# A transformer's root mean square norms: the root taken straight from the bank of the sums

## The chip, the cores and the metric

The kernel runs on one core of one Trainium2 chip. The metric is the device time of one execution in microseconds, as a median of several runs. TensorE does the matrix products, VectorE and ScalarE the elementwise work, GpSimd (POOL in the profile) some more of it, and SyncE (SP) issues most DMAs.

## The reference

One sequence of T = 512 tokens with D = 1024 features goes through three blocks, all in float32.

1. A first block: adaptive scale, shift and gate vectors from `c`; sliding window attention beside a gated short convolution, each with a norm of its own; an output projection; then a feed-forward part (FFN) with a convolution in its gate, and a norm at the end.
2. An RWKV-7 time mixing block and a SwiGLU FFN, each between two norms.
3. A block with a spatial gate (SGU) and a SwiGLU FFN, each between two norms.

Every norm over features is the same, with EPS = RMS_EPS = 1e-6:

```python
def rms_norm(x, g):
    xf = x.astype(jnp.float32)
    y = xf * lax.rsqrt(jnp.mean(xf * xf, axis=-1, keepdims=True) + EPS)
    return (y * g.astype(jnp.float32)).astype(x.dtype)
```

## The kernel before

**Layout.** The features lie on the 128 partitions, the tokens along the free dimension. An activation is a set of KD = 8 tiles of 128 by 512. Weights come as units of 128 output columns: `load` (L214) brings a unit into `raw`, `split_hi` (L226, ScalarE) rounds it into `whi`, `split_lo` (L232, VectorE) takes the rest into `wlo`, and TensorE makes three products for each tile (L247, L248, L249: high by high, high by low, low by high). Two slots of `whi` and `wlo` take turns, so the split of a unit waits until TensorE is done with the unit two before it.

**Order.** Every engine has its own program, written out by hand, and semaphores between them; an engine does its instructions strictly in the order of its program. There is no planner.

**A norm.** ScalarE squares the tiles (L300, L305 or L435), and TensorE multiplies the squares with a matrix of ones into bank 4 (`NORM_BANK`), which puts the sum over all features on every partition. `Norm` first adds most squares on GpSimd (`pool_add`, L317), and `pe_sums` (L329 to L340) ends with the product at L339 (L333 where the squares have slots of their own). `LeadNorm` sums tile by tile (`pe_sum_of`, L441), woven into the first two units of the next projection. Then come three steps on 128 by 512 elements:

- `dve_mean` (L344, L446), VectorE: `var` = sums / (n * 128) + eps, read from the bank;
- `act_root` (L326), ScalarE: `var` = sqrt(`var`), in place;
- `dve_rstd` (L351), VectorE: `rstd` = 1 / `var`.

The function table of ScalarE has to hold the square root when `act_root` runs; where ScalarE comes from another function, an ACT_TABLE_LOAD stands before it.

**The twelve norms, in order of time.** `norm1` (start), `norm_cv` and `norm_at` (convolution and attention, one after the other through the same bank, while TensorE runs the output projection), `ffn0.norm`, `norm_f` (closes the first block; together with the next block's norm, which `dve_both_norms` computes from the same sums through another root, L1578, and reciprocal, L1573), `out_tm.norm_o`, `ffn1.norm`, `ffn1.norm_o`, `norm_g` (the gate's), `out_gu.norm_o`, `ffn2.norm`, `ffn2.norm_o` (last in the kernel).

**What follows a norm.** `norm1` and `ffn0.norm` are followed by `Split`, which normalises tile after tile and makes the operands of TensorE. The norms named `norm_o` are followed by `Residual`: VectorE scales the output by `rstd` (L1235), adds it to `x` (L1240), and `Halves` makes `fh_hi` (L411, ScalarE) and `fh_lo` (L415, VectorE) of it, which TensorE waits for. In `ffn1`, `ffn2` and the gate the products are made before their norm is known, and VectorE multiplies the results by `rstd` afterwards (L1497, L3026); in the gate a gelu on ScalarE (L2974) comes before the next `split_hi` there.

**Setup.** `pool_setup` writes the constants on GpSimd, counted by `const_ready`; `pe_setup` waits for the tenth and then for number `MORE_CONSTS`.

Of the kernel before, what the change touches and what calls it, by code (L numbers as in the profile page):

```python
# [22 lines left out]
ALU = mybir.AluOpType  # L23
ACT = mybir.ActivationFunctionType
AX_X = mybir.AxisListType.X

P = 128
# [12 lines left out]
EPS = 1e-6  # L40
# [78 lines left out]
def build(nc, A, out):  # L119
# [3 lines left out]
    def sb(name, shape, dt=F32):  # L123
        return ctx.enter_context(nc.sbuf_tensor(name, shape, dt))
# [19 lines left out]
    mod = sb("mod", [P, 6 * KD])  # L144
    gain = sb("gain", [P, KD])
    cact = sb("cact", [P, KD])
    bank = [ctx.enter_context(nc.psum_tensor(f"bank{i}", [P, T], F32)) for i in range(8)]
    NORM_BANK, ADA_BANKS = 4, (7, 6, 6)

# [119 lines left out]
    sq_ready, acc_step, sum_step, sq_summed = count("sq_ready"), count("acc_step"), count("sum_step"), count("sq_summed")  # L269
# [4 lines left out]
    class Norm:  # L274
# [4 lines left out]
        def __init__(self, src, n, ready, eps=EPS, rstd_=None, var_=None, slots=None):  # L279
            self.src, self.n, self.ready, self.eps, self.slots = src, n, ready, eps, slots  # L280
            self.rstd = rstd[:, :] if rstd_ is None else rstd_
            self.var = var[:, :] if var_ is None else var_
            self.sq0, self.acc0 = sq_ready.claim(n), acc_step.claim(0 if slots else n - 2)
            self.sum0, self.var0, self.std0, self.rstd0 = (
                c.claim(1) for c in (sum_step, var_ready, std_ready, rstd_ready))

        def act_slot_free(self, act, k):
            if not isinstance(k, int):
# [33 lines left out]
                self.pool_add(pool, k)  # L322

        def act_root(self, act):
            act.wait_ge(var_ready.sem, self.var0 + 1)
            act.activation(self.var, self.var, ACT.Sqrt).then_inc(std_ready.sem, 1)  # L326

        def pe_sums(self, pe):
            wait(pe, var_ready.sem, self.var0)  # L329
            if self.slots is not None:  # L330
                for k in range(self.n):
                    pe.wait_ge(sq_ready.sem, self.sq0 + k + 1)
                    mm = pe.matmul(bank[NORM_BANK][:, :], ones[:, :], self.slots[k], start=k == 0, stop=k == self.n - 1)  # L333
                mm.then_inc(sum_step.sem, 1)
                return
            pe.wait_ge(acc_step.sem, self.acc0 + self.n - 2)
            pe.matmul(bank[NORM_BANK][:, :], ones[:, :], sq_sum[:, :], start=True, stop=False)
            pe.wait_ge(sq_ready.sem, self.sq0 + self.n)
            pe.matmul(bank[NORM_BANK][:, :], ones[:, :], sq[:, (self.n - 1) % 2, :], start=False, stop=True)\  # L339
              .then_inc(sum_step.sem, 1)  # L340

        def dve_mean(self, dve):
            dve.wait_ge(sum_step.sem, self.sum0 + 1)
            dve.tensor_scalar(self.var, bank[NORM_BANK][:, :], 1.0 / (self.n * P), self.eps,  # L344
                              ALU.mult, ALU.add).then_inc(var_ready.sem, 1)

        def dve_rstd(self, dve, mean=True):
            if mean:
                self.dve_mean(dve)
            dve.wait_ge(std_ready.sem, self.std0 + 1)  # L350
            dve.reciprocal(self.rstd, self.var).then_inc(rstd_ready.sem, 1)  # L351
            dve.wait_ge(rstd_ready.sem, self.rstd0 + 1)
# [69 lines left out]
    class LeadNorm(Norm):  # L422
# [3 lines left out]
        def __init__(self, src, n, ready):  # L426
            self.src, self.n, self.ready, self.eps = src, n, ready, EPS
            self.rstd, self.var = rstd[:, :], var[:, :]
            self.sq0, self.summed0 = sq_ready.claim(n), sq_summed.claim(n)
            self.var0, self.std0, self.rstd0 = (c.claim(1) for c in (var_ready, std_ready, rstd_ready))  # L430

        def act_square(self, act, k):
            self.ready(act, k)
# [2 lines left out]

        def pe_sum_of(self, pe, k):
            if k == 0:
                wait(pe, var_ready.sem, self.var0)
            pe.wait_ge(sq_ready.sem, self.sq0 + k + 1)  # L440
            pe.matmul(bank[NORM_BANK][:, :], ones[:, :], sq[:, k % 2, :], start=k == 0, stop=k == self.n - 1)\  # L441
              .then_inc(sq_summed.sem, 1)

        def dve_mean(self, dve):
            dve.wait_ge(sq_summed.sem, self.summed0 + self.n)
            dve.tensor_scalar(self.var, bank[NORM_BANK][:, :], 1.0 / (self.n * P), self.eps,  # L446
                              ALU.mult, ALU.add).then_inc(var_ready.sem, 1)


    w_in, w_o, ada_w = (A[n].rearrange("a k n -> (a k) n") for n in ("w_in", "w_o", "ada_w"))  # L450
# [35 lines left out]
    BY_DVE = [m for m in range(EARLY) if m not in ON_PE]  # L486
# [116 lines left out]
    def pool_setup(pool):  # L603
        pool.memset(ident[:, :], 0.0).then_inc(const_ready, 1)
        pool.memset(ones[:, :], 1.0).then_inc(const_ready, 1)
        pool.memset(rot[:, :], 0.0).then_inc(const_ready, 1)
        pool.memset(mask[:, :], 0.0).then_inc(const_ready, 1)
        pool.wait_ge(const_ready, 4)
        pool.affine_select(out=ident[:, :], in_=ident[:, :], compare_op=ALU.not_equal, fill=1.0, base=0,
                           pattern=[[-1, P]], channel_multiplier=1).then_inc(const_ready, 1)  # L610

        lower = rot[:, :].rearrange("p (h s m) -> p h s m", h=2, s=2)
        pool.affine_select(out=lower[:, :, 0, :], in_=lower[:, :, 0, :], compare_op=ALU.not_equal, fill=-1.0,
                           base=-32, pattern=[[-HD, 2], [-1, 32]], channel_multiplier=1).then_inc(const_ready, 1)
        pool.wait_ge(const_ready, 6)
        pool.affine_select(out=lower[:, :, 1, :], in_=lower[:, :, 1, :], compare_op=ALU.not_equal, fill=1.0,
                           base=0, pattern=[[-HD, 2], [-1, 32]], channel_multiplier=1).then_inc(const_ready, 1)

        pool.affine_select(out=mask[:, :], in_=mask[:, :], compare_op=ALU.is_ge, fill=MASKED, base=P,
                           pattern=[[-1, 2 * P]], channel_multiplier=1).then_inc(const_ready, 1)  # L620
        pool.wait_ge(const_ready, 8)
        pool.affine_select(out=mask[:, :], in_=mask[:, :], compare_op=ALU.is_gt, fill=MASKED, base=0,
                           pattern=[[1, 2 * P]], channel_multiplier=-1).then_inc(const_ready, 1)
        pool.memset(cbuf[:, :, 0:2], 0.0).then_inc(const_ready, 1)

        pool.memset(quarter[:, :], 1.0).then_inc(const_ready, 1)
        pool.memset(spread[:, :], 0.0).then_inc(const_ready, 1)
        pool.wait_ge(const_ready, 12)
        pool.affine_select(out=quarter[:, :], in_=quarter[:, :], compare_op=ALU.is_ge, fill=0.0, base=0,
                           pattern=[[1, P]], channel_multiplier=-32).then_inc(const_ready, 1)  # L630
        pool.wait_ge(const_ready, 13)
        pool.affine_select(out=quarter[:, :], in_=quarter[:, :], compare_op=ALU.is_ge, fill=0.0, base=31,
                           pattern=[[-1, P]], channel_multiplier=32).then_inc(const_ready, 1)
        copies = spread[:, :].rearrange("p (c m) -> p c m", m=32)
        for q in range(NT):
            pool.wait_ge(const_ready, 14 + q)
            pool.affine_select(out=copies, in_=copies, compare_op=ALU.not_equal, fill=1.0, base=-32 * q,
                               pattern=[[0, NT], [-1, 32]], channel_multiplier=1).then_inc(const_ready, 1)

    CONSTS, MORE_CONSTS = 10, 18  # L640

    def pe_setup(pe):
        pe.wait_ge(const_ready, CONSTS)
# [494 lines left out]
    def dve_mixer1(dve):  # L1138
        dve_positions(dve)
        for n in range(len(BY_DVE)):  # L1140
            if n == 2:
                dve_angles(dve)
            if n == len(BY_DVE) - 4:
                norm1.dve_mean(dve)
            if n == len(BY_DVE) - 3:
                norm1.dve_rstd(dve, mean=False)
            dve_early(dve, n)
        split_lo(dve, first[0])
        split_lo(dve, first[1])
# [19 lines left out]
            for k in range(half.n):  # L1169
                half.dve_lo(dve, k)  # L1170
        norm_cv.dve_rstd(dve)
        norm_at.dve_mean(dve)
        split_lo(dve, first[N_IN + 2])
        norm_at.dve_rstd(dve, mean=False)
        ada_add(dve, 1)
        for u in range(N_O):
            if u:
# [377 lines left out]
    norm_f = ffn0.norm_o  # L1555
# [3 lines left out]
    def dve_both_norms(dve):  # L1559
# [8 lines left out]
        dve.wait_ge(gsq_summed, 1)  # L1568
        dve.scalar_tensor_tensor(sq_sum[:, :], bank[GAINED_BANK][:, :], 1.0 / D, tmp[:, 0, :], ALU.mult, ALU.add)\
           .then_inc(both_step, 1)  # L1570
        norm_f.dve_mean(dve)
        dve.wait_ge(both_std, 1)
        dve.reciprocal(rstd[:, :], sq_sum[:, :]).then_inc(both_step, 1)  # L1573
        dve.wait_ge(both_step, 3)
# [5 lines left out]

    def dve_final(dve, k):
        if k == 0:
            norm_f.dve_rstd(dve, mean=False)
        dve.scalar_tensor_tensor(x[:, k, :], x[:, k, :], v("final", k), rstd[:, :], ALU.mult, ALU.mult)\
           .then_inc(x_normed, 1)

# [247 lines left out]
    class Steps:  # L1834
# [11 lines left out]
        def wait(self, eng, j, name, before=0):  # L1846

            wait(eng, self.sem, (j - before) * len(self.names) + self.names.index(name) + 1)
# [1405 lines left out]
```

## Time and profile before

| | |
|---|---|
| median of 3 runs | 2149.49 us (2148.24 to 2149.53) |
| the profiled execution | 2151.54 us, span 2149.4 us |
| TensorE busy | 1998.9 us, 93% |
| VectorE busy | 1079.3 us, 50% |
| ScalarE busy | 781.7 us, 36% |
| GpSimd busy | 239.3 us, 11% |
| mean granted TensorE clock | 0.957 |

The span runs from the first to the last instruction of the profiled execution; the execution's own time has some 2.1 us around it. An engine's busy share is a mean over stages, so it doesn't tell where the engine sets the pace. All times within the kernel count from the span's start. The granted clock is a share of TensorE's full 2.4 GHz; 0.50 is its lower level, 1.2 GHz.

### The profile page before, as it was taken

The page shows a single profiled execution, that of the slowest core. Times are in us where ns is not written, and L with a number is a line of the kernel's source. Part 1 is how long each engine was busy: PE and PEld are TensorE (multiplying, and loading weights), DVE is VectorE, ACT ScalarE, POOL GpSimd, SP SyncE. Part 2 cuts the span into 40 slices and gives each one's busy share as a digit, 9 for nine tenths or more (in the row PEclk, how much of TensorE's full clock was granted, in tenths as well). Part 3 has the DMA queues.
Part 4 walks back from the last instruction along what each step waited for, and adds up shares of the span by engine and source line. Part 5 has one row for each costly group of instructions (what it writes and reads, how often), then busy time and mean ns, then how long its engine had stood idle before and what let it go on. Part 6 is the DMA issues. An engine that isn't in the chain of part 4 may idle for free.

```text
span 2149.4 us, 35027 instructions
## 1 busy us (share of the span) xinstructions
PE 1998.9 (93%) x14351; PEld 1567.9 (73%) x14351; DVE 1079.3 (50%) x1579; ACT 781.7 (36%) x1237; POOL 239.3 (11%) x269
## 2 busy tenths in 40 slices
PE   6998989999997999889979899999979989999997
PEld 5776768888883677667757588888857858888885
DVE  6777765554325644677742644432264554444323
ACT  3334333333222334667623333322244343333221
POOL 1100000000014000322211011110100001111100
PEclk8999989999998999899989899999989989999998
DMA  9544223333331122000002133343222313333320
GB/s 297 165 129 128 79 69 88 97 95 106 103 89 52 59 88 73 6 9 9 5 26 69 55 93 96 98 120 95 80 59 70 88 49 98 98 98 105 108 81 39
DMA packets 311052, 181.02 MB, mean 84 GB/s; under 512 B 16381, under 2 KB 303763, under 8 KB 310932
## 3 DMA queue, kind: packets, MB, share of 16 engines
q1 hardware_dynamic: 305506, 162.29, 25.7%
q0 software_dynamic: 4608, 16.78, 2.5%
q8 instruction: 92, 1.51, 0.3%
q10 hardware_dynamic: 818, 0.21, 0.0%
q14 instruction: 28, 0.23, 0.0%
HBM read 177.16 MB, written 2.10 MB: 83 GB/s over the span
## 4 chain that ended last, share of the span: by engine, by line
PE 61%; issue 5%; DVE 4%; ACT 2%; POOL 1%; DVEq 0%; ACTq 0%; POOLq 0%
PE bank L247 16%; PE bank L249 15%; PE bank L248 15%; PE bank L1969 4%; PE bank L441 1%; PE bank L1759 1%; PE bank L2463 1%; PE bank L2457 1%; DVE rstd L351 1%; PE bank L2564 1%; POOL gsq L1449 1%; ACT whi L226 0%; PE bank L2674 0%; PE bank L2675 0%; PE bank L2649 0%
## 5 line engine op out<-in xcount | busy, mean ns | idle before, releaser
L232 DVE TENSOR_TENSOR wlo<-raw,whi 128x1024 fp32r<-128x1024 f32 (+1 forms) x262 | 340.2, 1299 | 723.1 <-ACT whi L226 723.0
L226 ACT ACTIVATE whi<-raw 128x1024 fp32r<-128x1024 f32 (+1 forms) x262 | 292.9, 1118 | 747.4 <-PE bank L249 740.2
L247 PE MATMUL bank<-fh_hi,whi 128*128 128x512 f32 x1056 | 421.0, 399 | 24.1 <-DVE fh_lo L415 16.8
L248 PE MATMUL bank<-fh_lo,whi 128*128 128x512 f32 x1056 | 415.0, 393 | 0.0
L249 PE MATMUL bank<-fh_hi,wlo 128*128 128x512 f32 x1056 | 414.9, 393 | 0.0
L247 PEld LDWEIGHTS bank<-fh_hi,whi 128*128 128x128 f32 x1056 | 199.2, 189 | 81.9 <-DVE fh_lo L415 27.7
L248 PEld LDWEIGHTS bank<-fh_lo,whi 128*128 128x128 f32 x1056 | 199.5, 189 | 44.8 <-issue 2.1
L249 PEld LDWEIGHTS bank<-fh_hi,wlo 128*128 128x128 f32 x1056 | 199.4, 189 | 44.4
L248 PE MATMUL bank<-f_lo,whi 128*128 128x512 f32 x528 | 205.4, 389 | 0.0
L247 PE MATMUL bank<-f_hi,whi 128*128 128x512 f32 x528 | 205.4, 389 | 0.0
L249 PE MATMUL bank<-f_hi,wlo 128*128 128x512 f32 x528 | 205.4, 389 | 0.0
L1541 POOL TENSOR_TENSOR sq<-sq,rstd 128x512 f32<-128x512 f32 x44 | 80.1, 1820 | 457.6 <-ACT sq L1404 457.6
L248 PEld LDWEIGHTS bank<-f_lo,whi 128*128 128x128 f32 x528 | 99.1, 188 | 20.8
L247 PEld LDWEIGHTS bank<-f_hi,whi 128*128 128x128 f32 x528 | 99.1, 188 | 20.6
L249 PEld LDWEIGHTS bank<-f_hi,wlo 128*128 128x128 f32 x528 | 99.1, 188 | 20.4
L2010 POOL TENSOR_TENSOR MTb<-MT,m_level 128x256 f32<-128x256 f32 x80 | 63.5, 821 | 346.0 <-DVE MT L2278 289.2
L1406 ACT ACTIVATE f_hi<-tmp 128x512 f32 (+1 forms) x66 | 41.7, 632 | 153.3 <-DVE tmp L1507 153.3
L247 PE MATMUL bank<-xs_hi,whi 128*128 128x512 f32 x192 | 79.6, 415 | 6.4 <-DVE xs_lo L1673 6.4
L249 PE MATMUL bank<-xs_hi,wlo 128*128 128x512 f32 x192 | 77.5, 403 | 0.0
L248 PE MATMUL bank<-xs_lo,whi 128*128 128x512 f32 x192 | 77.3, 403 | 0.0
L1510 DVE TENSOR_TENSOR f_lo<-tmp,f_hi 128x512 f32 (+1 forms) x66 | 45.7, 693 | 58.4 <-ACT f_hi L1406 58.4
L1507 DVE TENSOR_TENSOR tmp<-bank,sq 128x512 f32<-128x512 f32 x66 | 45.5, 689 | 55.0 <-POOL sq L1541 54.6
(418 smaller groups left out, 3102.6 us busy)
## 6 DMA issues: line engine op xcount, KB each, us to landing
raw<-in_w_up_dram SPq DMA_DIRECT2D x44, 512.0 KB, 3.8
raw<-in_ffn_w_gate_dram SPq DMA_DIRECT2D x44, 512.0 KB, 3.8
raw<-in_ffn_w_up_dram SPq DMA_DIRECT2D x44, 512.0 KB, 3.8
raw<-in_ffn_w_down_dram SPq DMA_DIRECT2D x32, 704.0 KB, 4.6
late<-in_ada_w_dram POOLq DMA_DIRECT2D x32, 512.0 KB, 4.2
raw<-in_rwkv_w_rkv_dram SPq DMA_DIRECT2D x24, 512.0 KB, 4.0
raw<-in_w_down_dram SPq DMA_DIRECT2D x16, 704.0 KB, 4.6
early<-in_ada_w_dram SPq DMA_DIRECT2D x16, 512.0 KB, 13.9
```

The costliest lines, as they stand in the source:

```text
L226: act.activation(whi[:, at.slot, 0:kts * P], raw_unit(at, kts), ACT.Copy).then_inc(hi_ready, 1)
L232: dve.tensor_tensor(wlo[:, at.slot, 0:kts * P], raw_unit(at, kts), whi[:, at.slot, 0:kts * P].bitcast(F32), ALU.subtract).then_inc(lo_read ...
L247: pe.matmul(dst, hi, rhs_hi(k), start=first and k == 0, stop=False)
L248: pe.matmul(dst, hi, rhs_lo(k), start=False, stop=False)
L249: mm = pe.matmul(dst, lo, rhs_hi(k), start=False, stop=last and k == kts - 1)
L351: dve.reciprocal(self.rstd, self.var).then_inc(rstd_ready.sem, 1)
L1406: act.activation(tile_at(self.f_hi, p), ft[:, q, :], ACT.Copy).then_inc(fhi_ready.sem, 1)
L1507: dve.tensor_tensor(ft[:, q, :], bank[2 * q + 1][:, :], acc[:, q, :], ALU.mult)\
L1510: dve.tensor_tensor(tile_at(self.f_lo, p), ft[:, q, :], tile_at(self.f_hi, p).bitcast(F32), ALU.subtract).then_inc(f_ready.sem, 1)
L1541: pool.tensor_tensor(sq[:, q, :], sq[:, q, :], rstd[:, :], ALU.mult).then_inc(s_scaled.sem, 1)
L1969: mm = pe.matmul(q[k][0], q[k][1], q[k][2], start=True, stop=True)
L2010: POOLm.done(pool.tensor_tensor(MTb[:, i % 2, e, :, :], MT[:, e, :, :], m_level[:, i + 1:i + 2, :].to_broadcast([P, NT, CH]), ALU.mult), f ...
```

## The change

VectorE's mean is given up. ScalarE's root reads the bank of the sums directly: its scale is 1 / (n * 128), and its bias a new column `eps_col` of 128 by 1, which GpSimd fills with EPS in the setup. The root waits for the sums, where it waited for the mean. TensorE's next sums into the bank wait for the root (`std_ready`) and no longer for the mean (`var_ready`). Where VectorE's mean and reciprocal stood apart in its program with other work between them, only the reciprocal is left, at its old place. The other norm of `dve_both_norms` and the layer norm in the gate stay as they were.

```diff
+    eps_col = sb("eps_col", [P, 1])
...
         def act_root(self, act):
-            act.wait_ge(var_ready.sem, self.var0 + 1)
-            act.activation(self.var, self.var, ACT.Sqrt).then_inc(std_ready.sem, 1)
+            act.wait_ge(sum_step.sem, self.sum0 + 1)
+            act.activation(self.var, bank[NORM_BANK][:, :], ACT.Sqrt, bias=eps_col[:, 0:1], scale=1.0 / (self.n * P))\
+               .then_inc(std_ready.sem, 1)
 
         def pe_sums(self, pe):
-            wait(pe, var_ready.sem, self.var0)
+            wait(pe, std_ready.sem, self.std0)
...
-        def dve_mean(self, dve):
-            dve.wait_ge(sum_step.sem, self.sum0 + 1)
-            dve.tensor_scalar(self.var, bank[NORM_BANK][:, :], 1.0 / (self.n * P), self.eps,
-                              ALU.mult, ALU.add).then_inc(var_ready.sem, 1)
-
-        def dve_rstd(self, dve, mean=True):
-            if mean:
-                self.dve_mean(dve)
+        def dve_rstd(self, dve):
             dve.wait_ge(std_ready.sem, self.std0 + 1)
             dve.reciprocal(self.rstd, self.var).then_inc(rstd_ready.sem, 1)
...
         def pe_sum_of(self, pe, k):
             if k == 0:
-                wait(pe, var_ready.sem, self.var0)
+                wait(pe, std_ready.sem, self.std0)
...
-        def dve_mean(self, dve):
-            dve.wait_ge(sq_summed.sem, self.summed0 + self.n)
-            dve.tensor_scalar(self.var, bank[NORM_BANK][:, :], 1.0 / (self.n * P), self.eps,
-                              ALU.mult, ALU.add).then_inc(var_ready.sem, 1)
+        def act_root(self, act):
+            act.wait_ge(sq_summed.sem, self.summed0 + self.n)
+            act.activation(self.var, bank[NORM_BANK][:, :], ACT.Sqrt, bias=eps_col[:, 0:1], scale=1.0 / (self.n * P))\
+               .then_inc(std_ready.sem, 1)
...
+        pool.memset(eps_col[:, :], EPS).then_inc(const_ready, 1)
+
+    CONSTS, MORE_CONSTS = 10, 19
...
-            if n == len(BY_DVE) - 4:
-                norm1.dve_mean(dve)
             if n == len(BY_DVE) - 3:
-                norm1.dve_rstd(dve, mean=False)
+                norm1.dve_rstd(dve)
...
         norm_cv.dve_rstd(dve)
-        norm_at.dve_mean(dve)
         split_lo(dve, first[N_IN + 2])
-        norm_at.dve_rstd(dve, mean=False)
+        norm_at.dve_rstd(dve)
...
-        norm_f.dve_mean(dve)
         dve.wait_ge(both_std, 1)
...
-            norm_f.dve_rstd(dve, mean=False)
+            norm_f.dve_rstd(dve)
```

## Rows read from the trace of the kernel before

**Rows 1.** The page, parts 1 and 4: busy times, and the chain by engine.

```profile
PE 1998.9 (93%) x14351; PEld 1567.9 (73%) x14351; DVE 1079.3 (50%) x1579; ACT 781.7 (36%) x1237; POOL 239.3 (11%) x269
...
PE 61%; issue 5%; DVE 4%; ACT 2%; POOL 1%; DVEq 0%; ACTq 0%; POOLq 0%
```

**Rows 2.** Tile `var`: line, operation, count; ns (min/median/max); first and last start.

```profile
L326 ACT ACTIVATE var<-var x11: 629/630/634, 32.2 to 2126.2; 128x512 f32<-128x512 f32 x11
L351 DVE RECIPROCAL rstd<-var x11: 3346/3353/3353, 32.8 to 2126.8; 128x512 f32<-128x512 f32 x11
```

**Rows 3.** Timeline at ffn0's norm: start, duration, instruction [idle before, releaser].

```profile
284.41 0.69 DVE L446 TENSOR_SCALAR var<-bank 128x512 f32<-128x512 f32 x1 [2.41 <-PE bank L441]
...
285.80 3.35 DVE L351 RECIPROCAL rstd<-var 128x512 f32<-128x512 f32 x1 [0.69 <-ACT var L326]
```

**Rows 4.** Timeline at out_tm's norm: the mean, and TensorE's restart.

```profile
1183.81 0.69 DVE L344 TENSOR_SCALAR var<-bank 128x512 f32<-128x512 f32 x1 [1.04 <-PE bank L339]
...
1191.67 0.80 PE L247 MATMUL bank<-fh_hi,whi 128*128 128x512 f32 x1 [7.89 <-DVE fh_lo L415]
```

**Rows 5.** Timeline at ffn1's closing norm.

```profile
1564.98 1.28 ACT L326 ACT_TABLE_LOAD   x1
...
1566.18 0.69 DVE L344 TENSOR_SCALAR var<-bank 128x512 f32<-128x512 f32 x1 [0.86 <-PE bank L339]
1566.91 0.63 ACT L326 ACTIVATE var<-var 128x512 f32<-128x512 f32 x1 [0.64 <-DVE var L344]
1567.57 3.35 DVE L351 RECIPROCAL rstd<-var 128x512 f32<-128x512 f32 x1 [0.70 <-ACT var L326]
```

**Rows 6.** Timeline at the gate's norm: the mean, and TensorE's two waits after it.

```profile
1595.52 0.69 DVE L446 TENSOR_SCALAR var<-bank 128x512 f32<-128x512 f32 x1 [0.67 <-PE bank L441]
...
1604.07 0.50 PE L247 MATMUL bank<-gh_hi,whi 128*128 128x512 f32 x1 [1.77 <-DVE wlo L232]
...
1615.77 0.84 PE L2905 MATMUL bank<-ident,o_gu 128*128 128x128 f32 x4 [2.06 <-ACT v_tk L2967]
```

**Rows 7.** Timeline at norm_cv and norm_at.

```profile
227.79 1.98 PE L333 MATMUL bank<-gb_sb,ones 128*128 128x512 f32 x4 [0.79 <-DVE var L344]
...
231.82 0.69 DVE L344 TENSOR_SCALAR prj<-bank 128x512 f32<-128x512 f32 x1
...
242.57 1.10 PE L441 MATMUL bank<-sq,ones 128*128 128x512 f32 x2 [0.16 <-ACT sq L435]
```

**Rows 8.** Timeline at norm1.

```profile
30.89 1.28 ACT L326 ACT_TABLE_LOAD   x1
32.18 0.63 ACT L326 ACTIVATE var<-var 128x512 f32<-128x512 f32 x1
```

**Rows 9.** Timeline at norm_f: the other norm's root and reciprocal.

```profile
672.17 0.63 ACT L1578 ACTIVATE sq_sum<-sq_sum 128x512 f32<-128x512 f32 x1 [6.60 <-DVE sq_sum L1569]
...
672.83 3.35 DVE L1573 RECIPROCAL rstd<-sq_sum 128x512 f32<-128x512 f32 x1
```

**Rows 10.** Groups of ScalarE by line and shape: count, busy us, mean ns, idle before.

```profile
L2974 ACT ACTIVATE o_gu<-tmp,vecs 128x512 f32<-128x512 f32 x16 | 11.5, 722 | 27.7 <-DVE tmp L3026 27.7
...
L865 ACT ACTIVATE prj<-bank,vecs 128x512 f32<-128x512 f32 x6 | 4.0, 671 | 0.0
```

**Rows 11.** Busy us (count) of PE, PEld, DVE, ACT, POOL; PEclk, DMA share, GB/s.

```profile
1213.00:1225.00 12.00, 12.00 (x54) 9.71 (x53) 8.88 (x8) 5.19 (x6) 1.54 (x1) 1.00 0.30 87
```

**Rows 12.** Timeline of the setup: GpSimd's last constants, TensorE's wait.

```profile
4.71 1.67 POOL L637 TENSOR_SCALAR_AFFINE_SELECT spread<-spread 128x128 f32<-128x128 f32 x4
...
8.84 0.76 PE L648 MATMUL bank<-pos_f,quarter 4*128 4x128 f32 x2 [4.91 <-DVE pos_f L678]
```

**Rows 13.** Stretches after three waits of TensorE, columns as in rows 11.

```profile
291.30:294.80 3.50, 3.20 (x7) 2.16 (x8) 3.50 (x7) 1.63 (x3) 0.00 (x0) 0.50 0.00 0
...
1191.70:1199.30 7.60, 7.10 (x13) 3.94 (x13) 5.97 (x10) 3.21 (x5) 0.00 (x0) 0.50 0.00 0
...
1615.80:1619.10 3.30, 3.30 (x11) 2.71 (x12) 1.38 (x2) 0.60 (x1) 0.00 (x0) 0.53 0.08 23
```

More of the change, by code:

```diff
@@ L283, in __init__ @@
             self.sq0, self.acc0 = sq_ready.claim(n), acc_step.claim(0 if slots else n - 2)
-            self.sum0, self.var0, self.std0, self.rstd0 = (
-                c.claim(1) for c in (sum_step, var_ready, std_ready, rstd_ready))
+            self.sum0, self.std0, self.rstd0 = (c.claim(1) for c in (sum_step, std_ready, rstd_ready))
         def act_slot_free(self, act, k):
@@ L429, in __init__ @@
             self.sq0, self.summed0 = sq_ready.claim(n), sq_summed.claim(n)
-            self.var0, self.std0, self.rstd0 = (c.claim(1) for c in (var_ready, std_ready, rstd_ready))
+            self.std0, self.rstd0 = (c.claim(1) for c in (std_ready, rstd_ready))
         def act_square(self, act, k):
@@ L638, in pool_setup @@
                                pattern=[[0, NT], [-1, 32]], channel_multiplier=1).then_inc(const_ready, 1)
-    CONSTS, MORE_CONSTS = 10, 18
+        pool.memset(eps_col[:, :], EPS).then_inc(const_ready, 1)
+    CONSTS, MORE_CONSTS = 10, 19
     def pe_setup(pe):
```

## The prediction

> **What bounds the kernel now.** I read the page first. TensorE is busy 93% of the span [rows 1], and the chain that ended last is 61% matmuls and only 4% VectorE [rows 1], so an edit on VectorE and ScalarE pays only where TensorE stands still for it. The busy times can't say where that is, so I took the tile `var` and its four lines next: eleven roots of 0.63 us on ScalarE, and eleven reciprocals of 3.35 us on VectorE [rows 2], with a mean of 0.69 us before each pair [rows 3]; the twelfth norm writes `prj` in place of `var`. Twelve norms, then. For each I read the timeline around its mean and asked two things: is TensorE idle until something that follows the reciprocal, and when could ScalarE have started the root. The reader should see one repeated figure: from the start of the mean to the start of the reciprocal go 1.39 us (284.41 to 285.80 [rows 3]; 1566.18 to 1567.57 [rows 5]): mean 0.69, hop 0.04, root 0.63, hop 0.03 [rows 5]. The mean is a link of its own in this chain, so taking it out shortens the chain by its time and one hop, if the root costs no more from the bank.
>
> **The change, part by part.**
>
> *The price of the new root.* Before, ScalarE reads SBUF with a plain bias. After, it reads a bank of 512 columns and takes its bias from a column `eps_col`. The nearest row is L865, bank to SBUF with a bias column: 0.67 us [rows 10]. The bounds are the old root itself, 0.63 us [rows 2], and L2974, SBUF to SBUF with a bias column, 0.72 us [rows 10]. I take 0.67. With the hop of 0.03 the reciprocal starts 0.70 us after the root starts. Where ScalarE is free when the sums end, 1.39 becomes 0.70: 0.69 us saved (0.64 to 0.73 by the bounds).
>
> *Where ScalarE is free and TensorE waits: three norms.* ffn0's first norm (284.41 [rows 3]), out_tm's norm (1183.81 [rows 4]) and the gate's norm (1595.52 [rows 6]). After out_tm's norm TensorE sits idle 7.89 us, until the first `fh_lo` made from the reciprocal [rows 4]. After the gate's norm it is less plain, since TensorE has units to work on; but it then waits 1.77 us for `wlo` at 1604.07 [rows 6]. ScalarE's queue is why: behind the root come the gelu, which needs the reciprocal's product, and only then the split that makes `whi`. 0.69 is less than 1.77, so all of it is passed on. 3 x 0.69 = 2.07 us.
>
> *Where a table load is in the way: three norms.* ffn1's, out_gu's and ffn2's closing norms, all of the pattern of rows 5. ScalarE comes from another function and loads the root's table when its last square is out. The load starts at 1564.98 and takes 1.28 us, so it ends at 1566.26, 0.08 us after the sums are ready at 1566.18 [rows 5]. It used to lie wholly beside the mean; with the mean gone 0.08 us of it shows, and 0.01 to the instruction behind it. 1.39 becomes 0.09 + 0.70 = 0.79: 0.60 us saved, 3 x 0.60 = 1.80 us. Behind two of them TensorE waits for the first split tile as above, and behind the last nothing hides VectorE's way to the output.
>
> *norm_cv and norm_at.* TensorE waits 0.79 us, until 227.79, to reuse the bank [rows 7]. It waited for the mean (0.69 after the sums), and waits for the root (0.67) after: nothing. norm_at's root comes about 1 us earlier, since ScalarE need not wait for VectorE's mean at 231.82, which stood behind the first reciprocal [rows 7]. TensorE works through its units meanwhile; of what follows only 0.16 us of idle time, before the sum at 242.57 that waits for a square [rows 7], can be won. 0.16 us.
>
> *The five that give nothing.* norm1: the root starts at 32.18, directly behind the table load that began at 30.89, with no idle time between, so it is ScalarE's own work that holds it and not the mean [rows 8]. norm_f: the reciprocal at 672.83 waits for the other root, ScalarE's at 672.17 for 0.63; the mean ran beside that one [rows 9]. ffn1's and ffn2's first norms: behind ffn1's mean TensorE is busy 12.00 of 12 us, and ffn2 repeats it [rows 11], so a reciprocal 0.69 us earlier ends in slack. With norm_cv above these are five norms.
>
> *What is added.* One GpSimd memset, before a constant that TensorE's setup waits for. GpSimd's last constant is done at 6.38 (4.71 plus 1.67), and the matmul behind that wait starts at 8.84, released by a cast of the positions [rows 12]. 2.4 us of cover for about 0.2 us: nothing. No DMA is added or moved. VectorE loses twelve instructions, 8.3 us, but is off the path elsewhere.
>
> *What waits now.* ScalarE's root waits for the sums themselves where it waited for the mean. Queued behind it are the splits of the next weights and the first `fh_hi`; the wait ends earlier than before in each case, so nobody behind it is later. TensorE's next sum into the bank waits for the root, and the previous root is long done everywhere but in norm_at.
>
> Sum: 2.07 + 1.80 + 0.16 = 4.03 us. The profiled execution took 2151.54 us, with a span of 2149.4; less 4.0 that is 2147.5. The median of the runs lies 2.05 lower, 2149.49, so I forecast 2149.49 - 4.03 = 2145.5 us.
>
> **A page against the row.** The three norms with a load rest on its 1.28 us [rows 5]. The Trainium skill, page "ScalarE: Activation LUTs", section "Rules for kernel authors", tells authors to budget about 2.7 us for every switch to another table set. By that figure the root could not start before 1567.68, later than it did before, the three norms would gain nothing and the sum would be 2.23. The trace speaks against it as it stands: the old root started 1.93 us after the load began.
>
> **The rivals.**
>
> *The load hides a tail.* In the kernel before 0.65 us pass between the load's end, 1566.26, and the root, 1566.91 [rows 5]. If ScalarE needs that time after a load, the three roots start when they did, and 1.80 us go: gain 2.23, time 2147.3. For it: no row of this line shows a root sooner with the mean in front. Against: norm1's root stands 0.01 us behind its load [rows 8]. The 2.7 us of the page above point this way.
>
> *The load moves behind the wait.* If it were issued only once the sums are there, three roots would start 1.29 after them, not 0.09: 3 x 1.20 = 3.6 us back, gain 0.43, time 2149.1. Against: the load that began at 1564.98 stood before its root's wait, since the root's data came only at 1566.87, the end of the mean [rows 5].
>
> *The clock is kinder.* After TensorE's idle time of 2.06 us at 1615.77 [rows 6] the granted clock is 0.53 over 3.3 us of full work [rows 13], mostly the lower level of 1.2 GHz; the idle 1.77 us at 1604.07 cost no such stretch. The second pause isn't shortened, but comes some 2.8 us earlier in the run. If the clock holds through it, 1.65 us come on top: gain 5.7, time 2143.8.
>
> *The clock is harsher (slower than before).* After the long waits the clock is at 0.50 for 3.5 us of TensorE's work in ffn0, but for 7.6 us in ffn1, from 1191.70 on [rows 13]. Half of what is lost at half clock is work: 4.1 us more of it cost 2.05. Resuming earlier could meet the chip at a worse moment; it decides from 8.1 us more at the lower level (half of that is the 4.03 gained). Were all four restarts that much worse: 8.2 - 4.0 = +4.2, time 2153.7. Against: the later restarts are already at the long end, so only ffn0's has far to fall.
>
> **How the numbers follow.** A measurement here tells about 0.2% from no change, 4.3 us, and my sum of 4.03 is 0.19%: just inside. Chances: forecast 0.62, kinder clock 0.17, hidden tail 0.09, load behind the wait 0.06, harsher clock 0.06. The forecast's own range is 2144.6 to 2146.5: six roots at 0.63 or 0.72 give +0.2 or -0.3, and a part of a clock stretch does the rest. About four tenths of it lie under 2145.2, so faster by over 0.2% gets 0.24 + 0.17 = 0.41; slower by over 0.2% only the harsher clock's worse part, 0.04; the rest, 0.55, is within. The range goes from the kinder clock to the hidden tail: 2143.8 to 2147.4.
>
> **What would show it.** Root durations of 0.67 and no L344 or L446; sums to reciprocal 0.70 at out_tm and 0.79 at the three norms with a load; TensorE's idle time before `fh_lo` 7.2 in place of 7.89, and before `wlo` 1.1 in place of 1.77; the same 3.35 reciprocals. It is wrong if a root over 0.72 shows, if a load stands between sums and root for over 0.1 us, or if the stretches at 0.50 clock add up to some 3 us more or less than before.

## The result, and the profile after

| | before | after |
|---|---|---|
| median | 2148.86 us (6 runs, 2146.83 to 2150.21) | 2162.37 us (6 runs, 2159.48 to 2169.41) |
| ratio | 1 | 1.0069, 95% [1.0054, 1.0085] |
| profiled execution | 2151.54 us, span 2149.4 | 2162.21 us, span 2160.5 |

The change makes the kernel 13.5 us slower by the medians, and 14.8 by the ratio (11.6 to 18.3 by its interval). The forecast was 2145.5, and the range ended at 2147.4.

The page of after, to be held against [rows 1]: the engines' busy times, the chain by engine, and two of the costliest groups (busy time, mean ns of one, then the idle time before them).

```profile
PE 2016.1 (93%) x14351; PEld 1565.0 (72%) x14351; DVE 1071.6 (50%) x1567; ACT 783.0 (36%) x1237; POOL 241.0 (11%) x270
...
PE 61%; issue 5%; DVE 5%; ACT 2%; POOL 1%; DVEq 0%; ACTq 0%; POOLq 0%
...
L248 PE MATMUL bank<-fh_hi,whi 128*128 128x512 f32 x1056 | 423.6, 401 | 22.7 <-DVE fh_lo L409 16.1
...
L248 PE MATMUL bank<-f_hi,whi 128*128 128x512 f32 x528 | 208.6, 395 | 0.0
```

VectorE is 7.7 us less busy, as it should be. But TensorE, which the change doesn't touch, is 17.2 us more busy (1998.9 before). That is the line to stop at.

The tile `var` of after, by line (count; shortest, median and longest in ns; first and last start), beside [rows 2]:

```profile
L326 ACT ACTIVATE var<-bank,eps_col x6: 669/687/688, 227.2 to 2137.1; 128x512 f32<-128x512 f32 x6
L440 ACT ACTIVATE var<-bank,eps_col x5: 687/689/690, 30.1 to 1775.0; 128x512 f32<-128x512 f32 x5
L345 DVE RECIPROCAL rstd<-var x11: 3343/3353/3353, 30.8 to 2137.9; 128x512 f32<-128x512 f32 x11
```

The timeline of after (start, duration, engine, line, in brackets the idle time before it and what ended it), at out_tm's norm, to be read against [rows 4]:

```profile
1176.73 1.12 PE L340 MATMUL bank<-sq,ones 128*128 128x512 f32 x2 [1.50 <-ACT sq L300]
1177.90 0.69 ACT L326 ACTIVATE var<-bank,eps_col 128x512 f32<-128x512 f32 x1 [1.22 <-PE bank L340]
1178.62 3.35 DVE L345 RECIPROCAL rstd<-var 128x512 f32<-128x512 f32 x1 [1.76 <-ACT var L326]
...
1185.08 0.79 PE L248 MATMUL bank<-fh_hi,whi 128*128 128x512 f32 x1 [7.22 <-DVE fh_lo L409]
```

The same view at ffn1's closing norm, against [rows 5], and at the gate's two pauses, against [rows 6]:

```profile
1568.33 1.28 ACT L326 ACT_TABLE_LOAD   x1
1568.36 1.12 PE L340 MATMUL bank<-sq,ones 128*128 128x512 f32 x2 [1.32 <-ACT sq L305]
1569.62 0.69 ACT L326 ACTIVATE var<-bank,eps_col 128x512 f32<-128x512 f32 x1
1570.34 3.35 DVE L345 RECIPROCAL rstd<-var 128x512 f32<-128x512 f32 x1 [1.68 <-ACT var L326]
1576.81 0.79 PE L248 MATMUL bank<-gh_hi,whi 128*128 128x512 f32 x1 [7.32 <-DVE gh_lo L409]
...
1605.69 0.50 PE L248 MATMUL bank<-gh_hi,whi 128*128 128x512 f32 x1 [0.93 <-DVE wlo L233]
...
1617.42 0.63 PE L2896 MATMUL bank<-ident,o_gu 128*128 128x128 f32 x4 [2.03 <-ACT v_tk L2958]
```

The norms do what was forecast. At out_tm the end of the sums (1176.73 + 1.12) lies 0.77 us before the reciprocal, and TensorE's pause is 7.22 in place of 7.89. Behind a table load the pause is 7.32. The pause for `wlo` is 0.93 in place of 1.77.

What is slower lies between the norms. The first product of ffn1's gate and up projections starts at 1185.08 here and at 1191.67 before [rows 4], so after is 6.59 us ahead. The first product that follows them, of after and then of before:

```profile
1442.82 0.39 PE L248 MATMUL bank<-f_hi,whi 128*128 128x512 f32 x1
```

```profile
1443.00 0.39 PE L247 MATMUL bank<-f_hi,whi 128*128 128x512 f32 x1
```

The lead is down to 0.18. The same products on the same engine took 257.74 us in place of 251.33. Two windows of 40 us, in ffn0's and in ffn1's gate and up projections (busy time and count of PE, then of PEld, DVE, ACT and POOL; granted clock, DMA share, GB/s), of before:

```profile
400.00:440.00 40.00, 40.00 (x173) 32.15 (x172) 20.07 (x25) 13.73 (x18) 0.00 (x0) 1.00 0.31 92
1320.00:1360.00 40.00, 40.00 (x178) 33.14 (x177) 15.89 (x19) 11.40 (x14) 7.21 (x4) 1.00 0.32 93
```

and of after:

```profile
400.00:440.00 40.00, 40.00 (x176) 32.83 (x175) 21.13 (x27) 13.57 (x18) 0.00 (x0) 1.00 0.32 92
1320.00:1360.00 40.00, 40.00 (x174) 32.11 (x173) 15.90 (x18) 12.84 (x16) 7.29 (x4) 1.00 0.31 92
```

The reader should see three things. TensorE has no idle time, full granted clock and the same DMA load in all four. In ffn1 it begins 174 products where it began 178. And in ffn0 it is the other way round: 176 now, 173 before. So the kernel before already had a slow stage, and the change exchanged which stages are slow.

I took the step, the time from one product's start to the next, in each stage (a product is 128 by 128 by 512 throughout). The table has its mean over the steps under 260 ns, which leaves out TensorE's waits and the steps of some 427 ns at the lower clock, and each stage's length from its first to its last product:

| stage, with its moving operand | step before, ns | step after, ns | length before, us | length after, us |
|---|---|---|---|---|
| first block's input and output projections, `h` | 228.4 | 233.1 | 226.1 | 229.7 |
| ffn0 gate and up, `fh` | 233.3 | 228.9 | 248.1 | 243.6 |
| time mix, `xs` | 233.3 | 229.8 | 173.9 | 171.2 |
| ffn0 down, `f` | 226.7 | 233.3 | 119.5 | 123.0 |
| time mix output, `ys` | 226.9 | 233.3 | 45.2 | 46.3 |
| ffn1 gate and up, `fh` | 226.8 | 233.3 | 251.1 | 257.5 |
| ffn1 down, `f` | 226.7 | 233.3 | 119.5 | 123.0 |
| gate, `gh` | 228.4 | 233.1 | 122.6 | 120.9 |
| gate output, `us` | 227.0 | 233.3 | 43.6 | 44.6 |
| ffn2 gate and up, `fh` | 226.8 | 233.3 | 250.8 | 257.3 |
| ffn2 down, `f` | 226.7 | 233.3 | 119.5 | 123.0 |

The lengths of `h` and of `gh` contain waits and stretches at the lower clock. The other nine stages together: 25.7 us longer in seven, 7.3 shorter in two, so 18.4 in all. `gh` gains 1.7 in spite of its step, through its shorter pause and the clock (below). `h` is 3.6 longer, which makes 20.3 for the whole table. The spans differ by 11.1. The norms outside the gate give back 3.0. Another 3.1 come from the first product, which starts at 46.74 for 49.84, and 3.1 from two stretches (before the time mix, and between it and its output). These last two items vary as much among the kernels without the change: there the first product starts between 45.5 and 49.8, and the two stretches take 26.4 to 28.2 and 269.0 to 276.1 us. So they aren't the change's.

What the change did to these stages: nothing but their place. `eps_col` is 4 bytes a partition, the allocator gives it 32, and it stands ahead of `vecs` and of every buffer of the stages. The byte addresses within a partition, as built:

```
buffer                    before (mod 512)   after (mod 512)
whi                        55424 (128)        55424 (128)     stationary
wlo                        66688 (128)        66688 (128)     stationary
h_hi, f_hi, gh_hi          97664 (384)        97696 (416)     moving
f_lo                      142720 (384)       142752 (416)
us_hi                     146816 (384)       146848 (416)
ys_hi                     174976 (384)       175008 (416)
fh_hi, ffn1 and ffn2      187776 (384)       187808 (416)
fh_lo, ffn1 and ffn2      204160 (384)       204192 (416)
xs_hi                     191392 (416)       191424 (448)
fh_hi, ffn0               191904 (416)       191936 (448)
fh_lo, ffn0               208288 (416)       208320 (448)
```

The weights stay and all moving operands go up by 32 bytes. The two stages that were slow before are the two that stood at 416.

### The profile page after: what moved, and what is told of

Read it like the earlier page. It is cut to its first block, busy times and chain, and to the rows that moved or that the text cites. A ratio compares the mean times of both kernels' runs of the same rounds, so it can differ in the third digit from the quotient of the medians.

```text
span 2160.5 us, 35015 instructions
## 1 busy us (share of the span) xinstructions
PE 2016.1 (93%) x14351; PEld 1565.0 (72%) x14351; DVE 1071.6 (50%) x1567; ACT 783.0 (36%) x1237; POOL 241.0 (11%) x270
## 4 chain that ended last, share of the span: by engine, by line
PE 61%; issue 5%; DVE 5%; ACT 2%; POOL 1%; DVEq 0%; ACTq 0%; POOLq 0%
PE bank L248 16%; PE bank L250 16%; PE bank L249 16%; PE bank L1960 4%; PE bank L435 1%; PE bank L1750 1%; PE bank L2454 1%; PE bank L2448 1%; DVE rstd L345 1%; PE bank L2555 1%; POOL gsq L1441 1%; ACT whi L227 0%; PE bank L2665 0%; PE bank L2666 0%; PE bank L2514 0%
## 5 line engine op out<-in xcount | busy, mean ns | idle before, releaser
L248 PE MATMUL bank<-fh_hi,whi 128*128 128x512 f32 x1056 | 423.6, 401 | 22.7 <-DVE fh_lo L409 16.1
L1499 DVE TENSOR_TENSOR tmp<-bank,sq 128x512 f32<-128x512 f32 x66 | 45.5, 689 | 55.6 <-POOL sq L1533 55.2
```

The lines of the kernel that those rows point to most:

```text
L248: pe.matmul(dst, hi, rhs_hi(k), start=first and k == 0, stop=False)
L1499: dve.tensor_tensor(ft[:, q, :], bank[2 * q + 1][:, :], acc[:, q, :], ALU.mult)\
```

## The experiments

Each was compared with the kernel before on the same chip. "Worth" is the ratio's distance from 1, times the median of before there.

Executions of one kernel differ mostly by the clock that they were granted. Of the 22 of before beside e9 to e12, those at a mean granted clock of 0.961 took 2142.0 to 2145.2 us, and those at 0.955 took 2150.9 to 2153.8. So the last column gives an estimate of the difference at equal clock: a straight line through the executions of both kernels, with one slope (it comes out as 1.3 to 1.6 us for each 0.001 of clock), with two standard errors.

| run | before, same chip, us | this, us (runs) | ratio [95%] | worth, us | at equal clock, us |
|---|---|---|---|---|---|
| e1 | 2145.89 (20 runs) | 2168.22 (5) | 1.0094 [1.0074, 1.0113] | +20.2 | +23.9 ± 1.9 |
| e2 | same | 2172.31 (4) | 1.0117 [1.0094, 1.0140] | +25.1 | +22.5 ± 2.5 |
| e3 | same | 2157.37 (7) | 1.0050 [1.0034, 1.0065] | +10.7 | +9.9 ± 1.6 |
| e4 | same | 2143.75 (12) | 0.9994 [0.9978, 1.0011] | -1.3 | -1.5 ± 1.4 |
| e5 | 2148.00 (24 runs) | 2142.64 (8) | 0.9973 [0.9961, 0.9984] | -5.8 | -4.0 ± 1.1 |
| e6 | same | 2141.39 (10) | 0.9978 [0.9964, 0.9992] | -4.7 | -4.8 ± 1.0 |
| e7 | same | 2150.93 (10) | 1.0007 [0.9995, 1.0020] | +1.5 | 0.0 ± 1.0 |
| e8 | same | 2177.21 (4) | 1.0130 [1.0111, 1.0150] | +27.9 | +28.5 ± 1.4 |
| e9 | 2146.91 (22 runs) | 2131.94 (6) | 0.9925 [0.9906, 0.9943] | -16.1 | -15.5 ± 1.4 |
| e10 | same | 2154.07 (9) | 1.0028 [1.0010, 1.0045] | +6.0 | +6.7 ± 1.2 |
| e11 | same | 2135.29 (6) | 0.9934 [0.9916, 0.9952] | -14.2 | -11.7 ± 1.2 |
| e12 | same | 2152.80 (10) | 1.0020 [1.0007, 1.0034] | +4.3 | +5.4 ± 1.4 |

The windows shown below are those of 400:440 (ffn0) and 1320:1360 (ffn1) again; all have clock 1.00.

### First: is it the place, and is it the place alone?

**e1.** The change, with everything behind `eps_col` 128 bytes up in place of 32.

```diff
-    eps_col = sb("eps_col", [P, 1])
+    eps_col = sb("eps_col", [P, 32])
...
-        pool.memset(eps_col[:, :], EPS).then_inc(const_ready, 1)
+        pool.memset(eps_col[:, 0:1], EPS).then_inc(const_ready, 1)
```

> The changed kernel, with eps_col 32 columns wide (128 bytes a partition) where it had one, which the allocator rounds to 32 bytes. Every buffer allocated after it then lies 128 bytes higher than in the kernel before, where eps_col of one column moves them by 32. Theory A (the start address of TensorE's moving operand sets the time of a product: 227 ns a product at a multiple of 128 bytes, 233 ns at 32 bytes past one): the products of ffn1 and ffn2 are back at 227 ns, and what is left is the gain of the shorter norms, about 4 us: 2145 us, ratio 0.998. Theory B (the new root or its waits slow the kernel, whatever the addresses): 2162 us, ratio 1.006, products at 233 ns.

```profile
400.00:440.00 40.00, 40.00 (x172) 32.15 (x172) 20.07 (x25) 13.10 (x17) 0.00 (x0) 1.00 0.33 97
1320.00:1360.00 40.00, 40.00 (x174) 32.43 (x173) 15.23 (x17) 11.41 (x15) 7.24 (x4) 1.00 0.33 97
```

The step is 232.4 ns in ffn1 and 234.3 in ffn0's first part. A shift by 128 doesn't bring the old rate back: the theory of a period of 128 bytes falls.

**e2.** The kernel before, with nothing but 32 unused bytes.

```diff
     cact = sb("cact", [P, KD])
+    pad = sb("pad", [P, 1])
```

> The kernel before, with an unused buffer of one column allocated where the change puts eps_col: the addresses of the changed kernel without its new root. Theory A: what the changed kernel lost, without its 4 us of gain: about 2166 us, ratio 1.008, products of ffn1 and ffn2 at 233 ns, those of ffn0's first part and of the time mix at 229 to 230. Theory B: no change, 2149 us, ratio 1.000.

```profile
400.00:440.00 40.00, 40.00 (x176) 32.84 (x175) 20.08 (x26) 14.21 (x19) 0.00 (x0) 1.00 0.33 96
1320.00:1360.00 40.00, 40.00 (x174) 32.11 (x173) 15.82 (x18) 11.47 (x14) 5.43 (x3) 1.00 0.34 97
```

No root, wait or memset is changed, and the windows are those of after: 176 and 174. The lengths of ffn0's and ffn1's gate and up are those of after too, to 0.2 us (243.6 and 257.3). It costs 25.1 us, 20.2 to 30.0 by its interval, and 22.5 at equal clock: its four executions had 0.954 to 0.958, and before's lay at 0.958 in the mean. Its lengths agree: 17.8 us more in the nine stages, and 3.0 in the first block's projections (229.1 for 226.1, both at a mean clock of 0.941). The gate is 0.8 shorter, since less of it ran at the lower clock; its 384 products at 233.2 ns for 228.4 cost 1.8. That is 22.6. The loss is explained by the rate.

**e3.** The same with 64 bytes: `pad = sb("pad", [P, 16])`.

> The kernel before, with an unused buffer of 64 bytes in the same place. Theory A, as the changed kernel's trace has it for the only two operands at 64 bytes past a multiple of 128 (229 to 230 ns): products at 230 ns in ffn1 and ffn2, at 233 in ffn0's first part and the time mix (96 past); about half of the loss at 32 bytes, 2161 us, ratio 1.005. A variant of it in which only multiples of 64 count: 227 ns in ffn1, no loss, 2149 us. Theory B: 2149 us.

```profile
400.00:440.00 40.00, 40.00 (x173) 32.16 (x172) 20.06 (x25) 13.89 (x19) 0.00 (x0) 1.00 0.31 92
1320.00:1360.00 40.00, 40.00 (x176) 32.84 (x175) 15.82 (x18) 11.90 (x15) 5.45 (x3) 1.00 0.34 98
```

ffn1 now has the step of 229.0 ns that ffn0 had 32 bytes ago: the rate goes with the address and not with the stage.

**e4.** The kernel before with `fh` of ffn0 and `xs` at a multiple of 512.

```diff
+                sbs(mem, "gpad", [P, 24])
...
+    sbs(shift_mem, "hpad", [P, 24])
```

> The kernel before, with 96 unused bytes behind gbuf and behind hb, so that fh_hi0, fh_lo0, xs_hi and xs_lo, the only large moving operands that lie at 32 bytes past a multiple of 128 there, start at a multiple of 128. Theory A: ffn0's first part and the time mix go from 233 to 227 ns a product: 1056 and 576 products of 6.6 ns less, 7.0 and 3.8 us, 2138 us, ratio 0.995. Theory B: 2149 us, ratio 1.000.

```profile
400.00:440.00 40.00, 40.00 (x173) 32.18 (x172) 20.21 (x25) 13.86 (x18) 0.00 (x0) 1.00 0.33 96
1320.00:1360.00 40.00, 40.00 (x178) 33.15 (x177) 16.37 (x18) 11.47 (x15) 6.66 (x4) 1.00 0.31 92
```

Nothing gained: the steps are 233.3 and 232.6 ns, so a multiple of 512 is about as slow as 416. An operand's own alignment isn't the rule. What was left was its distance to the weights, or its absolute place.

### Second: distance or place?

**e5.** The change without its new buffer: the constant goes into a last column of `vecs` that nobody uses.

```diff
-    eps_col = sb("eps_col", [P, 1])
...
+    eps_col = vecs[:, VB * P - 1:VB * P]
```

> The changed kernel with eps in the last, unused column of vecs, so that no buffer moves against the kernel before. Theory A2 (where TensorE's operands lie decides, but 128 bytes are not the period): products of ffn1 and ffn2 at 227 ns, and the 4.03 us of the forecast are left: ratio 0.998. Theory B (the new root or its waits slow the kernel): ratio 1.006 to 1.009, products at 233 ns.

Windows, and the timeline at out_tm's and at ffn1's closing norm:

```profile
400.00:440.00 40.00, 40.00 (x173) 32.10 (x173) 20.17 (x25) 13.85 (x18) 0.00 (x0) 1.00 0.33 96
1320.00:1360.00 40.00, 40.00 (x178) 33.10 (x177) 17.42 (x20) 12.42 (x16) 7.21 (x4) 1.00 0.31 92
```

```profile
1188.10 0.79 PE L248 MATMUL bank<-fh_hi,whi 128*128 128x512 f32 x1 [7.22 <-DVE fh_lo L409]
...
1560.79 1.28 ACT L326 ACT_TABLE_LOAD   x1
1562.09 0.69 ACT L326 ACTIVATE var<-bank,vecs 128x512 f32<-128x512 f32 x1
1562.81 3.35 DVE L345 RECIPROCAL rstd<-var 128x512 f32<-128x512 f32 x1 [1.68 <-ACT var L326]
```

The rates are those of before, and the kernel is faster: 5.8 us by the ratio, 3.4 to 8.4 by its interval, and 4.0 at equal clock. This is the forecast's sum of 4.03 measured by itself.

**e6.** The change with `eps_col = sb("eps_col", [P, 128])`, 512 bytes.

> The changed kernel with an eps_col of 512 bytes: every later buffer 512 bytes higher than before. In the runs so far products take 227 ns where the moving operand starts at 384 past a multiple of 512, 229 at 448, 232 to 234 at 0, 32, 416 and 480. Theory A2 with a period of 512 (or 256): 227 ns, ratio 0.998. If only one absolute place is good: 230 ns or more, ratio 1.005 or more. Theory B: 1.006 to 1.009.

```profile
1320.00:1360.00 40.00, 40.00 (x178) 33.15 (x177) 15.83 (x18) 12.42 (x15) 5.41 (x3) 1.00 0.34 100
```

Again 178, and 4.7 us faster than before. A whole 512 bytes change nothing.

**e7.** The kernel before with 128 bytes ahead of `raw`: weights and operands move together.

```diff
+    pad = sb("pad", [P, 32])
     raw = sb("raw", [P, RAW, HALF * P])
```

> The kernel before, with 128 unused bytes ahead of raw, so that the weights (whi, wlo) and the moving operands move together by 128. Theory R (what counts is the distance from the stationary operand to the moving one, 256 modulo 512 in the kernel before): no change, 227 ns, ratio 1.000. Theory S (what counts is the moving operand's own place): 232 to 233 ns as in the run with 128 bytes, some 20 us, ratio 1.010.

```profile
400.00:440.00 40.00, 40.00 (x173) 32.12 (x172) 20.86 (x27) 13.22 (x17) 0.00 (x0) 1.00 0.32 92
1320.00:1360.00 40.00, 40.00 (x178) 33.14 (x177) 16.36 (x18) 11.73 (x15) 6.41 (x4) 1.00 0.31 92
```

The operands went up by the same 128 bytes as in e1, and the rates are untouched, since the weights went with them. A rule of the absolute place falls.

**e8.** Only the weights move, by 128 bytes, and the operands by a whole 512.

```diff
     raw = sb("raw", [P, RAW, HALF * P])
+    pad = sb("pad", [P, 32])
     whi = sb("whi", [P, 2, HALF * P], F32R)
     wlo = sb("wlo", [P, 2, HALF * P], F32R)
+    pad2 = sb("pad2", [P, 96])
```

> The kernel before, with 128 unused bytes ahead of whi and 384 behind wlo: the weights at 256 modulo 512, the moving operands where they were modulo 512. Theory R: the distance is 128 in place of 256, products of ffn1 at 229 to 234 ns, 10 to 25 us, ratio 1.005 to 1.012. Theory S: no change, 227 ns, ratio 1.000.

```profile
400.00:440.00 40.00, 40.00 (x172) 32.18 (x171) 20.00 (x25) 13.67 (x18) 0.00 (x0) 1.00 0.32 92
1320.00:1360.00 40.00, 40.00 (x173) 32.15 (x173) 15.24 (x17) 11.45 (x15) 7.26 (x4) 1.00 0.33 96
```

Every stage is slow: 232.4 to 233.3 ns, and 234.1 to 234.3 in ffn0's first part and the time mix. With e7 this shows that it is the distance. And it is the distance to `whi` and `wlo`: `raw` stayed where it was, so its own distance to the operands is as before modulo 512.

### Third: use it, and take it apart

**e9.** e5, with `fh` of ffn0 and `xs` 480 bytes up, which puts them at the good distance too: `gpad` and `hpad` of e4 with `[P, 120]`.

> The changed kernel with eps in the last column of vecs, and 480 unused bytes behind gbuf and behind hb, which put fh_hi0, fh_lo0, xs_hi and xs_lo at 384 modulo 512, 256 past the weights, like the moving operands of all other stages. Theory R: ffn0's first part and the time mix go from 233.3 to 227 ns too: 1056 and 576 products, 7.0 and 3.8 us, less some that is hidden in the time mix; with the shorter norms ratio 0.993. Theory S with this place (384 modulo 512) says the same; if 96 or 480 bytes more between the buffers change nothing: 0.997.

```profile
400.00:440.00 40.00, 40.00 (x178) 33.14 (x177) 21.23 (x27) 13.73 (x19) 0.00 (x0) 1.00 0.32 92
1320.00:1360.00 40.00, 40.00 (x178) 33.14 (x177) 16.35 (x19) 11.66 (x15) 5.41 (x3) 1.00 0.36 104
```

178 products in both windows. It is the fastest version of the study, 15.0 us below the kernel before by the medians; its ratio to that kernel is 0.9925 where the change as made has 1.0069.

**e10.** The kernel before with ffn1's `fh_hi` and `fh_lo` alone 32 bytes up.

```diff
+                if tag == "1":
+                    sbs(part, "fpad", [P, 8])
```

> The kernel before, with 32 unused bytes ahead of fh_hi1 only: the moving operands of ffn1's gate and up products (and of nothing else) lie 32 bytes higher. Theory R: these 1056 products take 233.3 ns in place of 226.9, 6.8 us, everything else 227: ratio 1.003. If the loss came from something global (code, DMAs, another buffer that moved along): 1.000, 227 ns.

```profile
400.00:440.00 40.00, 40.00 (x173) 32.15 (x172) 20.87 (x27) 13.26 (x18) 0.00 (x0) 1.00 0.32 92
1320.00:1360.00 40.00, 40.00 (x173) 32.15 (x172) 15.19 (x17) 11.41 (x14) 7.23 (x4) 1.00 0.33 95
```

This stage takes 257.9 us in place of 251.1, and every other one is as before.

**e11.** The kernel before with `gpad` and `hpad` of e9.

> The kernel before, with the 480 unused bytes behind gbuf and behind hb alone. Theory R: 233.3 to 227 ns in ffn0's first part and the time mix, 7.0 + 3.8 = 10.8 us or somewhat less: ratio 0.995. The run with 96 bytes there (distance 384) kept 233 ns and 0.9994; if the place doesn't matter, this one repeats it.

```profile
400.00:440.00 40.00, 40.00 (x179) 33.10 (x177) 19.52 (x25) 15.02 (x20) 0.00 (x0) 1.00 0.34 99
1320.00:1360.00 40.00, 40.00 (x179) 33.10 (x178) 17.10 (x20) 11.51 (x14) 7.13 (x4) 1.00 0.32 92
```

ffn0's part goes from 248.1 to 241.3, the time mix from 173.9 to 170.8: 9.9 us by lengths. The medians lie 11.6 us apart, the ratio gives 14.2 (10.3 to 18.0), and at equal clock it is 11.7.

**e12.** The `fpad` of e10 between ffn1's `fh_hi` and `fh_lo`, so that only `fh_lo` moves.

> The kernel before, with 32 unused bytes between fh_hi1 and fh_lo1: one product in three of ffn1's gate and up part has a moving operand at distance 288 in place of 256. If each product pays for its own operand: 233 ns in that third, 2.3 us in all, ratio 1.001. If a product's read also meets the weight load for the next one, the neighbours' steps change too, and the mean over the three lies up to 233 ns: up to 6.8 us, 1.003.

The window, and four products in turn:

```profile
1320.00:1360.00 40.00, 40.00 (x175) 32.45 (x174) 16.26 (x19) 12.82 (x16) 7.22 (x4) 1.00 0.32 92
```

```profile
1330.17 0.40 PE L248 MATMUL bank<-fh_lo,whi 128*128 128x512 f32 x1
1330.41 0.39 PE L249 MATMUL bank<-fh_hi,wlo 128*128 128x512 f32 x1
1330.63 0.39 PE L247 MATMUL bank<-fh_hi,whi 128*128 128x512 f32 x1
1330.86 0.40 PE L248 MATMUL bank<-fh_lo,whi 128*128 128x512 f32 x1
```

The stage takes 255.1 us, 4.0 more: over half of e10's 6.8 with one product in three at the bad distance. The mean steps are 236.5 ns behind a product that moves `fh_lo`, 230.9 behind the one that comes ahead of it (`fh_hi` by `whi`), and 226.1 behind the third. So the moved operand costs in its own step and in the neighbour's.

## Why the prediction was wrong

**The step that failed** is "*What is added.* One GpSimd memset [...] nothing". The memset does cost nothing. But `eps_col` was added as well, and it wasn't costed: its place in memory moved TensorE's operands against the weights. Measured: the 32 bytes alone cost 25.1 us in e2 (20.2 to 30.0; 22.5 at equal clock), against 4.03 forecast as gained; of it 18.4 us stand in nine stages of after's own profile. e2 shows the loss without any of the change's work, and e5 and e6 show the work without the loss. Beside the same step's "No DMA is added or moved" a line on what the allocator moves should have stood.

The trace of before held the sign of it. I read windows for the clock only [rows 13] and never compared how many products TensorE begins in windows of equal clock and no idle time: 173 in ffn0 and 178 in ffn1. Two rates for one kind of product, from the same code lines, should have raised the question of what differs between the stages, and the place of the data is one such thing. The rival list was made of waits, loads and clock, and held nothing that acts on a busy TensorE.

**The price of the new root**: 0.69 us for 0.67, within the bounds of 0.63 to 0.72. **ScalarE free, TensorE waiting**: sums' end to reciprocal went from 1.43 (with the hop ahead of the mean) to 0.77 at out_tm, 0.66 saved for 0.69; TensorE's pause shrank by 0.67. **A table load in the way**: the pause shrank by 0.57 for 0.60. **norm_cv and norm_at**: TensorE waited 0.78 us for the bank in place of 0.79, norm_at's root started 3.74 us behind the first product of its sums (231.69 less 227.95) in place of 4.75, 1.0 us earlier as forecast, and the idle 0.16 us ahead of the later sum is gone. **The sum**: 4.03 us; e5 has 5.8 with an interval of 3.4 to 8.4 (4.0 ± 1.1 at equal clock), and e9 against e11, the same layout with and without the change's work, differ by 3.4 us in their medians. The mechanism and the size of the norms were right. **The gate** gained more than forecast: its first pause shrank by 0.84 for 0.69.

**The load hides a tail**: refuted. The root starts 0.01 us behind the load's end (1568.33 + 1.28 = 1569.61, root at 1569.62), though its sums had been ready since 1569.48. The 0.65 us of before were the wait for the mean. The Trainium skill's 2.7 us for a switch (page "ScalarE: Activation LUTs", section "Rules for kernel authors") isn't borne out here: 1.28 us is the whole of it. **The load moves behind the wait**: refuted by the same rows, the load starts 1.15 us ahead of the end of the sums.

**The clock is kinder**: seen in this execution. Windows of after behind the second pause of the gate and behind out_tm's norm, against [rows 13]:

```profile
1617.50:1620.80 3.30, 3.30 (x19) 2.80 (x20) 1.35 (x2) 0.77 (x2) 0.00 (x0) 1.00 0.07 21
...
1185.10:1192.70 7.60, 7.10 (x13) 3.97 (x13) 5.96 (x10) 3.22 (x5) 0.00 (x0) 0.50 0.00 0
```

After a pause of 2.03 us the granted clock stayed at 1.00 and TensorE began 19 operations in 3.3 us; before it was 0.53, with 11. e5's profiled execution shows 1.00 there too, those of e6, e9 and e11 show 0.51, 0.50 and 0.53. And e2, the kernel before with 32 unused bytes, has 1.00 behind its pause of 2.03 us, as has e3 behind one of 2.06:

```profile
1625.90:1629.20 3.30, 3.30 (x19) 2.80 (x20) 1.38 (x2) 0.71 (x2) 0.00 (x0) 1.00 0.07 19
```

So it goes with the execution and not with the change. Over the whole span TensorE ran at 0.50 for some 176 us here and some 185 before, worked out from the mean clocks; the sign "some 3 us more or less" shows, but kernels without the change range from 172 (e10) to 200 (e2), so it can't tell anything. **The clock is harsher**: not seen; behind out_tm's pause it is 7.6 us at 0.50 as before. The kernel came out slower, as that rival had it, but by another mechanism; that is no merit of the rival.

**What stays open.** Why the distance counts was not shown. That a weight load and a moving read of neighbouring products disturb each other in the memory would fit e12, where the neighbour pays too, but it is only argued. A distance of 0 wasn't tried. That 128 and 384, and 160 and 416, gave the same steps suggests a period of 256 bytes, on two pairs only. The distance doesn't say all either: in e1 ffn1's and ffn2's down products have their operands at the same addresses, and their steps are 232.4 and 233.3 ns.

norm1's root starts at 30.06 us here for 32.18 before. In both its table load starts directly behind ScalarE's copy into `vecs`, and that copy came 2.1 us earlier here. e7, without the change, has the root at 30.48 and its first product at 45.5, so this isn't owed to the change.

## What to carry to other kernels

A new buffer is part of a change, however small: list what the allocator moves behind it, or put the constant where nothing moves (an unused column, or the end of memory). Where TensorE sets the pace, count the products it begins in windows of equal clock and no idle time, stage by stage; two rates for one shape point at the operands' addresses, and here setting them right was worth 11.7 us at equal clock (14.2 by the ratio), about three times the change's own idea. Where executions spread, look at the granted clock of each before reading a small difference. And read a comparison that contradicts a sound sum as a question about what else was changed.

## What the runs showed of the hardware

For a product of 128 by 128 by 512 in float32 at full clock, streamed without idle time, the step depends on the distance between the start of the moving operand and the start of the weights' buffer, modulo 512 bytes (mean steps under 260 ns; the first block's projections and the gate, with their waits, are left out):

| distance | step, ns | seen in |
|---|---|---|
| 128 | 232.4 to 233.3 | e8 |
| 160 | 234.1 to 234.3 | e8's ffn0 and time mix |
| 256 | 226.7 to 227.5 | before, e4 to e7, e9 to e12 |
| 288 | 233.2 to 233.3 | before's ffn0 and time mix, after, e2, e10 |
| 320 | 228.9 to 229.8 | after's and e2's ffn0 and time mix, e3 |
| 352 | 233.3 to 233.4 | e3's ffn0 and time mix |
| 384 | 232.4 to 233.3 | e1, e4's ffn0 and time mix |
| 416 | 234.2 to 234.3 | e1's ffn0 and time mix |

The step from best to worst is 3.4%, and over a kernel that is 93% TensorE it came to 27.9 us in e8 (28.5 at equal clock). All starts here are multiples of 32 bytes. The Trainium skill (page "SBUF — State Buffer", section "Operand start alignment") asks only that a start be a multiple of the element's size, and says that this is about legality and not about speed; these runs put a price beside it.

The second surprise is how close ScalarE follows its table load: 0.01 us in after (1569.62 behind 1569.61) and 0.02 in e5, with the data already there. The third is how far the granted clock explains the spread: from 0.961 to 0.955 the kernel before takes some 9 us more.
